# Retention queries and keys turned through memory, weights in block order, and the norm's root on three columns

## What is computed

```
(sh1,sc1,g1,sh2,sc2,g2) = silu(c) @ w_ada + b_ada          # one set per sequence
h = rmsnorm(x) * (1 + sc1) + sh1
u = h @ w_in     # retention q,k,v,gate | attention q,k,v | two merge gates
A: retention, 8 heads, q and k rotated (rotary), decayed scores, recurrent state
B: banded attention, 8 heads, normed q and k, cache of 256 keys per sequence
x = x + g1 * ((sig(m_r) * yA @ w_br_ret + sig(m_a) * yB @ w_br_att) @ w_out)
x = x + g2 * (relu(rmsnorm(x)*(1+sc2)+sh2 @ w_up)^2 @ w_down)
```

## Time and profile before

| | |
|---|---|
| median of 3 runs | 1806.72 us (1802.99 to 1807.86) |
| the profiled execution | 1803.19 us |
| its span | 1801.2 us |
| TensorE clock granted, mean | 0.998 of full speed |
| PE busy | 1782.5 us (99%) |
| PEld busy | 1624.8 us (90%) |
| DVE busy | 994.8 us (55%) |
| ACT busy | 736.0 us (41%) |
| POOL busy | 353.4 us (20%) |
| chain that ended last | PE 97%, DVE 1%, ACT 1%, issue 1% |
| q1, the DMAs of SP | 484992 packets, 292.13 MB, 56.3% of the 16 engines' span |
| q0, the DMAs of POOL | 12592 packets, 44.99 MB, 7.7% |

### The profile page before, as it was taken

One profiled execution on the slowest core, in us unless ns is written; L12 is line 12 of the kernel. 1 busy time (PEld: TensorE's weight loads), 2 busy tenths in 40 slices (PEclk: granted clock), 3 DMA queues, 4 the chain that ended last, 5 costly groups with the idle time before them and its releaser, 6 DMA issues.

```text
span 1801.2 us, 35393 instructions
## 1 busy us (share of the span) xinstructions
PE 1782.5 (99%) x11933; PEld 1624.8 (90%) x11933; DVE 994.8 (55%) x1606; ACT 736.0 (41%) x1411; POOL 353.4 (20%) x459
## 2 busy tenths in 40 slices
PE   8999999999999999999999999999999999999998
PEld 7888888889999999999988888888899999999998
DVE  5466666667433575543364666666674346655333
ACT  3444444446222344532234444444463234554222
POOL 3333333330000120000023334333300004000000
PEclk9999999999999999999999999999999999999999
DMA  9878898896666734455638779888865635344432
GB/s 343 232 200 215 225 239 231 231 236 199 210 211 208 260 95 127 129 177 200 218 104 237 204 215 230 231 224 240 231 220 165 211 118 199 117 128 125 132 125 99
DMA packets 505240, 348.47 MB, mean 193 GB/s; under 512 B 201931, under 2 KB 468109, under 8 KB 505110
## 3 DMA queue, kind: packets, MB, share of 16 engines
q1 hardware_dynamic: 484992, 292.13, 56.3%
q0 software_dynamic: 12592, 44.99, 7.7%
q10 hardware_dynamic: 7526, 9.58, 1.5%
HBM read 313.56 MB, written 34.37 MB: 193 GB/s over the span
## 4 chain that ended last, share of the span: by engine, by line
PE 97%; DVE 1%; ACT 1%; issue 1%; ACTq 0%; POOL 0%; DVEq 0%
PE G L1591 50%; PE G L1627 32%; PE X L1752 8%; PE X L1650 2%; PE X L1551 2%; PE G L1861 2%; PE X L1627 1%; DVE wlo L1093 0%; PE X L1644 0%; DVE hp L1164 0%; DVE rstd L1154 0%; ACT hp L791 0%; ACTq L766 0%; ACT whi L772 0%; DVE hlo L1169 0%
## 5 line engine op out<-in xcount | busy, mean ns | idle before, releaser
L1093 DVE TENSOR_TENSOR wlo<-raw,whi 128x1024 fp32r<-128x1024 f32 x369 | 471.0, 1277 | 546.0 <-ACT whi L772 543.9
L772 ACT ACTIVATE whi<-raw 128x1024 fp32r<-128x1024 f32 x369 | 390.9, 1059 | 761.8 <-PE G L1591 442.3
L1627 PE MATMUL G<-whi,hhi 128*128 128x512 f32 x832 | 333.9, 401 | 1.7 <-DVE hlo L1169 1.4
L1627 PE MATMUL G<-whi,hlo 128*128 128x512 f32 x832 | 325.0, 391 | 0.0
L1627 PE MATMUL G<-wlo,hhi 128*128 128x512 f32 x832 | 324.5, 390 | 0.1
L1591 PE MATMUL G<-hhi,whi 128*128 128x384 f32 x704 | 236.8, 336 | 0.0
L1591 PE MATMUL G<-hhi,wlo 128*128 128x384 f32 x704 | 235.4, 334 | 0.0
L1591 PE MATMUL G<-hlo,whi 128*128 128x384 f32 x704 | 235.3, 334 | 0.0
L1627 PEld LDWEIGHTS G<-whi,hhi 128*128 128x128 f32 x832 | 156.2, 188 | 49.2 <-issue 13.1
L1591 PE MATMUL G<-ysp,whi 128*128 128x384 f32 x768 | 196.9, 337 | 0.0
L1627 PEld LDWEIGHTS G<-wlo,hhi 128*128 128x128 f32 x832 | 156.1, 188 | 34.1 <-DVE wlo L1093 0.6
(11 more groups left out here) (237 smaller groups left out, 2545.3 us busy)
## 6 DMA issues: line engine op xcount, KB each, us to landing
raw<-in_w_in_dram SPq DMA_DIRECT2D x256, 128.0 KB
raw<-in_w_in_dram SPq DMA_DIRECT2D x128, 256.0 KB
raw<-in_w_up_dram SPq DMA_DIRECT2D x64, 512.0 KB
raw<-in_w_down_dram SPq DMA_DIRECT2D x64, 512.0 KB
raw<-in_w_in_dram SPq DMA_DIRECT2D x49, 512.0 KB
ada_w<-in_w_ada_dram SPq DMA_DIRECT2D x44, 512.0 KB, 6.1
kc<-in_cache_attn_k_dram SPq DMA_DIRECT2D x64, 256.0 KB, 6.7
vc<-in_cache_attn_v_dram SPq DMA_DIRECT2D x32, 512.0 KB, 7.5
```

The source lines that it names most:

```text
L772: return a.activation(out, in_, ACT.Copy)
L1093: v.tensor_tensor(wlo[:, j % SPLIT, :, :], raw[:, j % RAW, :, :], whi[:, j % SPLIT, :, :].bitcast(F32), ALU.subtract).then_inc(blk_split, 1)
L1627: ins = t.matmul(B[banks[m][0]][:, :], x[:, kp * WK + k, m * P:(m + 1) * P], w[:, k, :], start=first and k == 0 and x is hhi and w is w_hi ...
```

## The change

1. **Weights in block order.** The host lays all 368 blocks out in the order in which they are used (`blocks`, the same numbers in another order). Each load is one DMA of 512 KB that reads 4 KB per partition.
2. **Rotated q and k through memory.** PE's six transposes per head, DVE's copy `qrT` and ACT's copy `krT` go. SP writes `qkR` (384 KB) to memory before its load of block 3 of the next turn, and behind that load waits for the write and reads it back by four DMAs in pieces of 128 bytes into `rkT`. DVE turns `rkT` in 32 x 32 squares, 128 x 768 in one instruction, behind `low(c, 1)`, then forms `qr_par`, and then `keys_low`, which moves here from the end of the turn before. PE waits for `rk_turned` ahead of the retention scores.
3. **The norm.** PE multiplies each 128 x 128 piece of the squares by one column of ones, so that the token's sum stands on its own partition: three columns in place of 384. ACT takes the root of 128 x 3, DVE the reciprocal of 128 x 3 and a diagonal matrix (`std_diag`), PE spreads it by three products with ones, and DVE copies the result from PSUM to `rstd`. Part of PE's modulation products goes ahead of the norm's, and the unused products behind the last norm are halved.
4. **The order around the norm.** POOL scales only four tiles ahead of the wait for `rstd`, and DVE forms the low part of tile 0 ahead of `hp` of tile 2.

```diff
-        def load(c, j, parts, into=None):
+        def load(c, j, n):
             sp.wait_ge(blk_split, c.blk + (j + 1))
             sp.sem_inc(load_go, 1)
...
+            sp.dma_start(raw[:, j % RAW, :, :].rearrange("p k n -> p (k n)"),
+                         w_blk[bass.ds(n, 1)].rearrange("a p n -> p (a n)")).then_inc(raw_full[j % RAW], 64)
...
+        def rotated_out(c, l, h):
+
+            sp.wait_ge(rope_ready, c.head)
+            sp.dma_start(rq_d[bass.ds(l * HEADS + h, 1)].rearrange("s a p d -> p (s a) d"),
+                         qkR[:, :, :].rearrange("p t (a d) -> p (t a) d", a=2)).then_inc(rq_out, 16)
+
+        def rotated_back(c, l, h):
+
+            sp.wait_ge(rq_out, c.head * 16)
+            for m in range(4):
+                src = rq_d[bass.ds(l * HEADS + h, 1), :, :, 32 * m:32 * m + 32]
+                sp.dma_start(rkT[32 * m:32 * m + 32, :, :].rearrange("j a (q i) -> j (a q) i", i=32),
+                             src.rearrange("s a (q j) i -> j (s a q) i", j=32)).then_inc(rk_full, 16)
...
                 for j in range(4):
+                    if prev is not None and j == 3:
+                        rotated_out(c, l, prev)
+                    load(c, j, h * 8 + (l * BLOCKS + B_HEAD + j))
+                if prev is not None:
+                    rotated_back(c, l, prev)
...
-            pool.wait_ge(tr_done, H)
+            pool.wait_ge(rq_out, H * 16)
...
-            act.wait_ge(tr_done, H + 1)
-            copy(krT[:, :], X[1][:, 0:TOK]).then_inc(kr_ev, 1)
...
-            v.reciprocal(rstd[:, PR:TOK], std[:, PR:TOK]).then_inc(rstd_ready, 1)
-            v.reciprocal(rstd[:, 0:PR], std[:, 0:PR]).then_inc(rstd_ready, 1)
+            c.op(v.reciprocal(rstd[:, 4:4 + NT], rstd[:, 0:NT]))
+            c.settle()
+            v.tensor_tensor(std_diag[:, :, :], ident[:, :].unsqueeze(1).to_broadcast([P, NT, P]),
+                            rstd[:, 4:4 + NT].unsqueeze(2).to_broadcast([P, NT, P]), ALU.mult).then_inc(diag_ready, 1)
+            dve.wait_ge(spread_done, c.norm + 1)
+            v.tensor_copy(rstd[:, PR:TOK], X[0][:, PR:TOK]).then_inc(rstd_ready, 1)
+            v.tensor_copy(rstd[:, 0:PR], X[0][:, 0:PR]).then_inc(rstd_ready, 1)
...
+        def rotated_turned(c):
+
+            dve.wait_ge(rk_full, c.head * 64)
+            tiles = rkT[:, :, :].rearrange("p a t -> p (a t)")
+            v.transpose(tiles, tiles).then_inc(rk_turned, 1)
+            dve.wait_ge(rk_turned, c.head)
...
             low(c, 1)
             if prev is not None:
+                rotated_turned(c)
+                keys_low(c)
                 probabilities(c)
                 decayed(c)
...
-            t.matmul(X[0][:, 0:TOK], ones[:, :], sq_sum[:, :], start=True, stop=False)
-            for n in range(2):
-                pe.wait_ge(sq_ready, c.norm * KT + (KT - 1 + n))
-                t.matmul(X[0][:, 0:TOK], ones[:, :], sq[:, n, :], start=False, stop=(n == 1)).then_inc(sq_used, 1)
+            mm(X[0][:, TOK:TOK + NT], ones[:, :], qr_par[:, 0, ST:ST + NT], stop=False)
+            for n in range(NT):
+                mm(X[0][:, TOK + n:TOK + n + 1], sq_sum[:, n * P:(n + 1) * P], ones[:, 0:1], start=False, stop=False)
+            for k in range(2):
+                pe.wait_ge(sq_ready, c.norm * KT + (KT - 1 + k))
+                for n in range(NT):
+                    ins = mm(X[0][:, TOK + n:TOK + n + 1], sq[:, k, n * P:(n + 1) * P], ones[:, 0:1], start=False, stop=(k == 1))
+                ins.then_inc(sq_used, 1)
+
+        def std_spread(c):
+
+            pe.wait_ge(diag_ready, c.norm + 1)
+            for n in range(NT):
+                ins = mm(X[0][:, n * P:(n + 1) * P], ones[:, :], std_diag[:, n, :])
+            ins.then_inc(spread_done, 1)
...
-            pe.wait_ge(qr_ev, c.head)
-            pe.wait_ge(kr_ev, c.head)
-            mm(X[0][:, 0:256], krT[:, 0:P], qrT[:, 0:2 * P])
+            pe.wait_ge(rk_turned, c.head)
+            mm(X[0][:, 0:256], rkT[:, 1, :], rkT[:, 0:3:2, :])
...
-            pe.wait_ge(rope_ready, H + 1)
-            for n in range(NT):
-                turned(X[0][:, n * P:(n + 1) * P], qkR[:, n, 0:DH])
-            for n in range(NT):
-                ins = turned(X[1][:, n * P:(n + 1) * P], qkR[:, n, DH:2 * DH])
-            ins.then_inc(tr_done, 1)
...
             if l:
                 with cnt.turn({"norm": 1}, use=("norm", "head")) as c:
+                    ada_products(ADA_GAP)
                     norm(c)
-                    ada_products(ADA_GAP)
-                    pe.wait_ge(std_ready, c.norm + 1)
+                    std_spread(c)
+                    pe.wait_ge(rstd_ready, c.norm * 2 + 2)
                     ada_products(ADA_GAP + 1)
...
+                pe.wait_ge(pair_ev, c.head * 4 + P0)
+                last_modulation(l, 0)
                 norm(c)
-            last_modulation(l)
+                std_spread(c)
+            for f in range(1, ADA_F + 1 - l):
+                last_modulation(l, f)
+            for _ in range(4 * l):
+                mm(X[3][:, 0:P], ones[:, :], ident[:, :])
```

More of the change, by code:

```diff
@@ L251, in trunk @@
     kaT = sb("kaT", [P, TOK], stack=hstack)
-    qrT = sb("qrT", [P, SEQ + P], stack=hstack)
-    krT = sb("krT", [P, TOK], stack=hstack)
+    rkT = sb("rkT", [P, 2 * NT, P], stack=hstack)
     vaT = sb("va_tok", [P, NT, AW], stack=hstack)
@@ L537, in _ @@
                     for j in range(4):
-                        load(c, j, [rows(w_out, l, j % 2, i * (2 * BC) + j // 2 * BC)])
+                        load(c, j, l * BLOCKS + B_OUT + i * 4 + j)
                         if i:
@@ L557, in _ @@
                     for j in range(8):
-                        load(c, j, [rows(w_down, l, j, i * BC)])
+                        load(c, j, l * BLOCKS + B_DOWN + i * 8 + j)
                         if l < DEPTH - 1 and j == DOWN_SENT[min(i, 1)]:
@@ L1176, in normed_tiles, with tile_low @@
         def normed_tiles(c, shift, k0, k1, block=None, at=None, free=None):
+            def tile_low(m):
+                dve.wait_ge(hhi_ready, c.norm * KT + (m + 1))
+                if m == k0 and free is not None:
+                    dve.wait_ge(ada_used, free)
+                c.op(sample_low(m))
+                prompt_low(shift, m).then_inc(h_ready, 1)
             for k in range(k0, k1 + 2):
@@ L1184, in normed_tiles @@
                     scaled(k)
-                if k >= k0 + 2:
-                    m = k - 2
-                    dve.wait_ge(hhi_ready, c.norm * KT + (m + 1))
-                    if m == k0 and free is not None:
-                        dve.wait_ge(ada_used, free)
-                    c.op(sample_low(m))
-                    prompt_low(shift, m).then_inc(h_ready, 1)
+                if k > k0 + 2:
+                    tile_low(k - 2)
         def first_modulation(c, part):
@@ L1273, in probabilities @@
             v.tensor_copy(pT[:, 2 * P:4 * P], X[3][:, 0:2 * P]).then_inc(pt_d, 1)
+        def rotated_turned(c):
[3 more added lines that the diff above has]
+            dve.wait_ge(rk_turned, c.head)
+            dve.wait_ge(dec_full, c.head * 16)
+            row = dec[:, DC_ROW:DC_ROW + 64].rearrange("p (g t) -> p g t", g=4)
+            c.op(v.tensor_tensor(par(qr_par[:, 0, :], 0), par(rkT[:, 4, :], 0), row, ALU.mult))
+            v.tensor_tensor(par(qr_par[:, 1, :], 1), par(rkT[:, 4, :], 1), row, ALU.mult).then_inc(qr_ev, 1)
         def scores_low(c):
@@ L1831, in merge, with last_modulation @@
                         j += 1
-        def last_modulation(l):
-            for f in range(ADA_F + 1 - l):
-                pe.wait_ge(adaf_full[f], l * 32 + 32)
-                for k in range(KT):
-                    ins = ada_product(X[1 + f], k, adaf_w[:, f, k, :], k == 0, k == KT - 1)
-                ins.then_inc(ada_mm, 1)
-            for _ in range(8 * l):
-                mm(X[3][:, 0:P], ones[:, :], ident[:, :])
+        def last_modulation(l, f):
+            pe.wait_ge(adaf_full[f], l * 32 + 32)
+            for k in range(KT):
+                ins = ada_product(X[1 + f], k, adaf_w[:, f, k, :], k == 0, k == KT - 1)
+            ins.then_inc(ada_mm, 1)
         def up(c):
```

148 lines of the change are left out of this document (85 added, 63 removed).

## The result

| | before | after |
|---|---|---|
| median of the runs | 1805.2 us (4 runs, 1803.0 to 1807.9) | 1870.6 us (4 runs, 1861.5 to 1875.4) |
| ratio | 1 | 1.036, 95% interval 1.0332 to 1.0388 |
| profiled execution, its span | 1803.2, 1801.2 us | 1872.3, 1870.8 us |
| mean granted clock of TensorE | 0.998 | 0.981 |

What follows compares the result with a forecast made beforehand. PE was taken to bound the kernel, busy 1782.5 of 1801.2 us. Products -10.6, waits +4.0 and norms -1.2 gave -7.8 us, 1799 us against the 1806.72 median; 8-in-10 range 1793 to 1827 us.

Steps and rivals of the forecast that it cites:

- Heads, what goes: In each head, PE's six transposes of qkR go: 0.66 us off the chain, 10.6 us over 16 heads.
- The write's issue: On SP's queue in a head turn, the write of qkR goes out behind three block loads, at 178.1 us.
- When the read-back lands: In the followed head turn, at 190.1 us, about 0.25 late with late starts: 4.0 us of PE waits in 16 heads.
- The figure of 2.9 us for half a trip: Skill's figure for write and read-back each: landing at 183.9, no wait; set aside because other transfers stand ahead.
- POOL's state transfers starve the trip: Rival: in the heads, POOL's state store and load delay the trip, 2.25 us a head, 1831 us; chance 0.27.
- The argument that q1 with rows of 4 KB would hold its own against POOL's store: Point against the starving rival: q1 had only small pieces in the earlier window, now rows of 4 KB.
- The wash: Rival: the queue drains at some 350 GB/s, landing at 191.5; head waits cancel the gains, 1807 us; chance 0.25.
- Blocks: Weight loads in the heads: 0 alone, but cover of the trip; without them the write goes out over 7 us later.
- Norms: The three norms' chains together: -1.2 us, between -3.5 and +1.
- The sign that the prediction named: Second norm of layer 1: wrong if its first product of h comes no sooner than 6.2 us behind the root.

Runs made afterwards that it cites:

- trip2_br: The change with the norms of before; SyncE issues the y_ret read-back, write and read-back between the next head's blocks two and three: 1797.6 us, ratio 0.9947.
- quiet: The change with POOL's stores and loads of the sample states cut to one eighth: 1833.6 us, ratio 1.0176.
- n_only: The kernel before with only the norms' part of the change: 1810.7 us, ratio 1.0030.
- b_only: The kernel before with only the weights laid out in block order: 1803.4 us, ratio 0.9995.
- r_only: The kernel before with only the rotated q and k turned over memory, weights not in block order: 1939.5 us, ratio 1.0742.
- write_first: The change with SyncE issuing the write of qkR ahead of the three weight blocks instead of behind them: 1879.9 us, ratio 1.0427.
- n_fill: The kernel before with the norms' part and five filler products ahead of PE's wait for the diagonals: 1808.7 us, ratio 1.0023.

## Why the prediction was wrong

- **Heads, what goes: right.** 0.66 us a turn, shown by the turns of 43.41 us in `trip2_br`.
- **The write's issue: right.** 178.1 forecast, 178.44 measured.
- **When the read-back lands: the step that failed.** Forecast 190.1 and 0.25 us of wait a head, with a bound of 2.1; measured 194.24 in that turn and 47.1 / 16 = 2.9 us on average. The mechanism was right, its size was not, in two terms. The first is the rate: the estimate let 3.73 MB pass at 390 GB/s, because the blocks come in rows of 4 KB. The engines moved 274, 336 and 303 GB/s in the three stretches of 4 us between the write's issue and its landing, 304 on average, which is below even the 326 that I had as the lower bound. At 304 the 3.73 MB take 12.3 us instead of 9.6:

```profile
178.00:182.00 4.00, 4.00 (x33) 3.04 (x31) 1.83 (x4) 1.06 (x1) 3.00 (x5) 1.00 0.88 274
182.00:186.00 4.00, 4.00 (x25) 3.14 (x18) 3.57 (x8) 2.39 (x9) 0.00 (x0) 1.00 1.00 336
186.00:190.00 4.00, 4.00 (x19) 3.34 (x18) 3.33 (x8) 2.23 (x5) 0.00 (x0) 1.00 0.75 303
```

  The second is that the estimate let the read-back follow when the bytes ahead had drained. It can't: SyncE first waits for the write's landing, then issues four DMAs in 2.04 us, and the last lands 2.76 us behind that, 4.4 us where the sum had 3.1. The two terms, 2.7 and 1.3 us, make up 4.0 of the 4.1 us between 190.1 and 194.24. Only in that worst turn is the write itself so late; in the usual one it lands after 7.8 us, with the same three blocks ahead of it.
- **The figure of 2.9 us for half a trip.** The Trainium skill, DMA: Bandwidth & Descriptors, section Anatomy of one DMA, gives it for DMAs that POOL issues, while these are SyncE's. The runs agree with it where nothing stood ahead of the write, 2.9 us (median) in `trip2_br`, and not in the change, 7.8. Setting it aside was right.
- **The clock: no term at all.** 25 us, priced in two ways and seen in one turn. This is what took the time out of reach of every rival.
- **The rival "POOL's state transfers starve the trip"** named the right place and had 0.27. It gave 2.25 us a head, of which 2.0 through these transfers; with them cut the wait fell by 29 / 16 = 1.8 us. That this is so near 2.0 is in part luck: the rival had the store ahead of the write by 2.6 us, and in `quiet` the write's median moved by 0.5 us, the read-back's by 1.3. It missed the clock, and so ended at 1831. Queue shares from 182 to 186 us, and then from 186 to 190, while the write was still out:

```profile
q1 hardware_dynamic: 931, 1.06, 81.1%
q0 software_dynamic: 98, 0.27, 17.3%
...
q0 software_dynamic: 245, 0.94, 58.1%
q1 hardware_dynamic: 114, 0.26, 16.9%
```

  The last stretch is the picture of the earlier trace rows, but the one before it is not. The argument that q1 with rows of 4 KB would hold its own against POOL's store stood until 186 us. Then 0.26 MB of q1 took 4 us beside the store, and the write landed at their end.
- **The wash** has a slip of its own: a landing at 191.5 is 1.4 us behind 190.1, not 1.2 at most. It changes nothing here.
- **Blocks: right.** Alone 0.9995 (0.9986 to 1.0004), and as cover of the trip 1939 less 1870.6, which is 69 us and the norms' 6 more. I had put 7 us a head on the later issue and measured 7.7. That TensorE would wait as much longer was too much: 4.1 us a head, since the write then landed sooner.
- **Norms: wrong in sign.** Forecast -1.2, bound +1; measured +5 to 6. The chain of `n_only` at the second norm of layer 1, to hold against the earlier trace rows:

```profile
1523.77 1.88 PE X L1689 x64
1525.65 2.34 PE X L1791 x20
...
1529.13 0.94 PE X L1791 x6
1530.07 3.40 PE X L1689 x64
1533.47 1.19 PE X L1791 x8
```

  The narrow products take 2.34 us, where I had taken 1.6 for ten of them and bounded 2.6. The heavier error: the modulation products of the earlier trace rows lay beside the root and the reciprocals before and cost nothing. Now half of them, and two thirds at the norm of layer 0, stand behind the spread and are themselves what ends last, at a lowered clock: 3.40 us for 64, where 64 took 1.88 at full clock. I had given the norms with products left behind the spread -0.2 each, as if these ended near the same time as before. The sign that the prediction named is there too: 6.65 us from the root to the first product of h in `n_only` (1528.01 to 1534.66), against 6.2.
- **The sum by what was measured:** -10.6 (products) + 47.1 (wait) + 25 (clock) + 5.9 (norms: the time from a stage's last product to the first product of h grew by 2.0, 2.3 and 1.6 us) - 1 (blocks) = +66; measured +65.3. That it closes is no proof of the clock's 25, which were themselves taken from what was left over.

## What to carry to other kernels

A trip through memory that ends in a wait of the bound engine is to be timed as issue, landing, issue and landing again, each behind the traffic of that moment, at the rate read where the same queues are busy together and not at the best rate of the trace. Add the clock to the price of such a wait: here 47 us of waits, 2.9 us a head, brought 25 us more. And before such a trip is dropped, try the queue's order: the same DMAs in another order were worth 67 to 70 us here (1870.6 less the norms' 6, against 1797.6 or 1794.7).

## What the runs showed of the hardware

- Rows of 4 KB were a little faster by the byte than rows of 1 KB when one queue filled the engines: 346 GB/s at share 1.00 in `b_only`, with SyncE's queue alone at work, beside 326 at share 1.01 in the earlier trace rows. With the write's rows of 512 bytes among them the changed kernel had 336 at share 1.00:

```profile
397.00:399.00 2.00, 2.00 (x10) 1.69 (x9) 1.17 (x2) 0.00 (x0) 1.98 (x4) 1.00 1.00 346
```

- The time to issue a DMA was not constant: the same four DMAs of 128-byte pieces took 2.04 us to issue in the change, 5.06 to 6.96 in `trip2_br` and `r_only`, and 10.48 behind four blocks in `write_first`.
- After an idle stretch of 4.0 us the granted clock was 0.50 for about 5 us, though TensorE worked without pause in them. In the next turn it fell to 0.50 behind an idle stretch of 2.4 us:

```profile
246.00:248.00 2.00, 2.00 (x6) 1.60 (x5) 2.00 (x4) 0.63 (x1) 0.55 (x1) 0.50 1.07 256
```

- The clock fell from 1.00 to 0.60 without any idle time behind one-column products (`n_fill`), and stayed at 1.00 through 0.9 us of idle in the kernel before.
